# An encoder trunk on one core: the norms at the four stage borders done by halves of the tokens

## The chip and the metric

The kernel runs on one core of a Trainium2 chip. The metric is the device time of one execution in microseconds; the number to be predicted is the median over several executions.

## What is computed

Two layers over 1024 tokens of width 1024 in float32. Each layer is a token mixer and a gated MLP, both added to the residual stream x, with an RMS norm ahead of each; one last norm ends the trunk. Layer 0 mixes with multi-head latent attention, layer 1 with differential attention.

```python
def rmsnorm(x, g=None):
    x32 = x.astype(jnp.float32)
    y = x32 * lax.rsqrt(jnp.mean(x32 * x32, axis=-1, keepdims=True) + NORM_EPS)
    ...

def conv_ffn(h, w_up, conv_w, conv_b, w_down):
    u = h @ w_up                              # 1024 -> 2 x 2816
    ...                                       # depthwise convolution, width 3
    g, val = jnp.split(u, 2, axis=-1)
    return (jax.nn.silu(g) * val) @ w_down

def reference(...):
    for i in range(DEPTH):                    # DEPTH = 2
        h = rmsnorm(x, attn_norm_g[i])
        x = x + mixer(h)                      # mla_mixer, then diff_mixer
        x = x + conv_ffn(rmsnorm(x, ffn_norm_g[i]), ...)
    return rmsnorm(x, final_norm_g)
```

## The kernel before

The stream x lies in SBUF as eight tiles k of 128 features by 1024 tokens; a half is 512 tokens (left, right). Each engine has its own instruction order, written out by hand, with semaphores between; there is no scheduler. A product in float32 takes three matmuls (`passes`, `three_passes`): each operand is split into a high part, rounded by ScalarE (ACT) (`split_high`, `norm_high`), and a low part, the difference, taken by GpSimd (POOL) or VectorE (DVE) (`split_low`, `norm_low`; of the norm's tiles POOL has the even ones and DVE the odd ones).

The stages are: latent attention; the projection of its output (`project_phase`, tiles named `mo_`); the MLP (`ffn_phase`, `ffn_ps` is its PSUM); differential attention; its projection (`do_`); the second MLP; the final norm (`fin_`). Between two stages stands a barrier of all engines. The stage borders that the change touches are numbered 1 (projection `mo_` to MLP 0), 2 (MLP 0 to differential attention), 3 (projection `do_` to MLP 1) and 4 (MLP 1 to the final norm). At each the same chain runs: last product; last residual add (DVE); its square (ACT); square sums over the 128 partitions by matmuls with ones (L272, `norm_sum_halves`); mean (L212), root (ACT L177), reciprocal (L218), both on columns of 128 tokens; the change of stage; a spread of these values over the partitions by matmuls with the identity (L285, `norm_spread`); and then, tile by tile, scale (DVE L231), high part (ACT L183), low part (L196), each half of a tile for itself, left halves first. The first product waits for tile 0.

The projection makes eight output tiles m; `unit(m)` does the left half's 24 matmuls, then the right half's. During its last tiles ACT and POOL also prepare the next stage's up weights (`UpAhead`: the value's tile, the gate's tile, and the sums S1, S2, S4 of weight blocks, added by POOL at L704, L707 and L710). x is written to DRAM as it is finished (`spill`).

The MLP goes through 22 pairs of output tiles. The first pair is an ordinary product over eight k (`first_pair`, left halves of both tiles first). From the second on, blocks are combined by a scheme with seven products in place of eight: it needs sums and differences T1 to T4 of blocks of normed x (DVE L1143, high parts on ACT L957, low parts on DVE L1133 and POOL L1070) and of weight blocks (`block_high` L715 on ACT, `block_low` L720 on POOL). These start when the whole norm is done. The down projection runs in 11 steps g (`groups`); a step has 16 units of six matmuls, one for each output tile and half, each added to x by DVE (L1200). Behind the last step ACT squares, POOL adds the squares and splits the next stage's first weights.

The stage calls end at the barriers that the trace shows as L2738 (into MLP 0), L2743, L2750 and L2754.

## Time and profile before

| | |
|---|---|
| median of three runs | 2862.83 us |
| the runs | 2861.6, 2862.83, 2864.22 us |
| the profiled execution, its span | 2863.4 us |
| TensorE (PE) busy | 2741.2 us, 96% |
| VectorE (DVE), ScalarE (ACT), GpSimd (POOL) busy | 1779.9, 1355.9, 1455.6 us |
| DMA | 195.37 MB, 68 GB/s |

The profile is one execution. Its page gives busy times by engine; the trace behind it gives every instruction with its start, its duration, and what ended the idle time before it. Every time in this text that starts with "at" is a moment of this execution, in us from its start.

### The profile page before, as it was taken

The page shows a single profiled execution, that of the slowest core. Times are in us where ns is not written, and L with a number is a line of the kernel's source. Part 1 is how long each engine was busy: PE and PEld are TensorE (multiplying, and loading weights), DVE is VectorE, ACT ScalarE, POOL GpSimd, SP SyncE. Part 2 cuts the span into 40 slices and gives each one's busy share as a digit, 9 for nine tenths or more (in the row PEclk, how much of TensorE's full clock was granted, in tenths as well). Part 3 has the DMA queues.
Part 4 walks back from the last instruction along what each step waited for, and adds up shares of the span by engine and source line. Part 5 has one row for each costly group of instructions (what it writes and reads, how often), then busy time and mean ns, then how long its engine had stood idle before and what let it go on. Part 6 is the DMA issues. An engine that isn't in the chain of part 4 may idle for free. (4 is left out here: it accounts for less than half of the span.)

```text
span 2863.4 us, 40261 instructions
## 1 busy us (share of the span) xinstructions
PE 2741.2 (96%) x13708; PEld 2306.7 (81%) x13708; DVE 1779.9 (62%) x2481; ACT 1355.9 (47%) x2102; POOL 1455.6 (51%) x1119
## 2 busy tenths in 40 slices
PE   8999999999989999999989999999898999999998
PEld 6788888877878888788868888887787788887886
DVE  6577777773654554555478888888527545545555
ACT  5477777773444444311246665665414444443112
POOL 2355555552587777643543333332226877774443
PEclk9999999999999999999999999999899999999998
DMA  3000000003122222523020000000321212225221
GB/s 137 23 9 11 9 7 7 17 1 135 72 89 72 82 88 88 198 89 117 15 113 23 30 30 31 30 23 24 153 96 35 105 68 86 88 79 215 88 88 59
DMA packets 54395, 195.37 MB, mean 68 GB/s; under 512 B 6544, under 2 KB 9872, under 8 KB 53776
## 3 DMA queue, kind: packets, MB, share of 16 engines
q1 hardware_dynamic: 54288, 193.95, 18.6%
q8 instruction: 66, 1.08, 0.1%
q14 instruction: 41, 0.34, 0.0%
HBM read 148.84 MB, written 45.09 MB: 68 GB/s over the span
## 5 line engine op out<-in xcount | busy, mean ns | idle before, releaser
L1209 PE MATMUL ffn_ps<-ffn_b_hi,weights_hi 128*128 128x512 f32 x704 | 277.5, 394 | 20.1 <-POOL weights_lo L720 11.7
L1210 PE MATMUL ffn_ps<-ffn_b_lo,weights_hi 128*128 128x512 f32 x704 | 276.1, 392 | 0.0
L1211 PE MATMUL ffn_ps<-ffn_b_hi,weights_lo 128*128 128x512 f32 x704 | 275.8, 392 | 0.0
L360 POOL TENSOR_TENSOR weights_lo<-weights_raw,weights_hi 128x1024 fp32r<-128x1024 f32 (+2 forms) x65 | 127.5, 1967 | 216.3 <-ACT weights_hi L355 216.2
L1100 POOL TENSOR_TENSOR ffn_y_lo<-ffn_y_raw,ffn_y_hi 128x1024 fp32r<-128x1024 f32 x44 | 109.1, 2498 | 229.4 <-ACT ffn_y_hi L1030 229.4
L720 POOL TENSOR_TENSOR up_local_lo<-up_sums,up_local_hi 128x512 fp32r<-128x512 f32 x126 | 171.2, 1362 | 96.9 <-ACT up_local_hi L715 96.9
L2301 ACT ACTIVATE dif_p<-dif_s,dif_neg_max 128x1024 f32<-128x1024 f32 x128 | 142.1, 1113 | 124.9 <-DVE dif_neg_max L2487 114.5
L1209 PE MATMUL ffn_ps<-ffn_b_hi,up_local_hi 128*128 128x512 f32 x504 | 196.1, 389 | 0.0
L1210 PE MATMUL ffn_ps<-ffn_b_lo,up_local_hi 128*128 128x512 f32 x504 | 196.1, 389 | 0.0
L1211 PE MATMUL ffn_ps<-ffn_b_hi,up_local_lo 128*128 128x512 f32 x504 | 196.1, 389 | 0.0
L1030 ACT ACTIVATE ffn_y_hi<-ffn_y_raw 128x1024 fp32r<-128x1024 f32 x44 | 44.2, 1052 | 315.0 <-PE ffn_ps L1211 315.0
L1200 DVE TENSOR_TENSOR x_first<-x_first,ffn_ps 128x512 f32<-128x512 f32 x176 | 120.4, 687 | 111.9 <-PE ffn_ps L1211 111.9
L1200 DVE TENSOR_TENSOR x_second<-x_second,ffn_ps 128x512 f32<-128x512 f32 x176 | 120.4, 687 | 111.9 <-PE ffn_ps L1211 111.9
L715 ACT ACTIVATE up_local_hi<-up_sums 128x512 fp32r<-128x512 f32 x126 | 79.0, 632 | 230.2 <-PE ffn_ps L1211 150.4
L1853 DVE TENSOR_REDUCE mat_row_max<-lat_s 128x1 f32<-128x1024 f32 x128 | 156.2, 1220 | 39.4 <-PE lat_s L371 38.3
L1706 ACT ACTIVATE mat_pt_hi<-mat_turn 128x512 fp32r<-128x512 f32 x256 | 138.8, 594 | 85.6 <-PE mat_turn L1979 85.4
L2390 POOL TENSOR_TENSOR dif_q_lo<-dif_rotated,dif_q_hi 64x512 fp32r<-64x512 f32 x64 | 85.0, 1329 | 177.0 <-ACT dif_q_hi L2283 173.2
L1209 PEld LDWEIGHTS ffn_ps<-ffn_b_hi,weights_hi 128*128 128x128 f32 x704 | 133.3, 189 | 51.6 <-issue 16.6
L1868 DVE TENSOR_TENSOR mat_pt_lo<-mat_turn,mat_pt_hi 128x512 fp32r<-128x512 f32 x256 | 162.7, 678 | 4.8 <-ACT mat_pt_hi L1706 4.8
L1148 DVE SCALAR_TENSOR_TENSOR ffn_conv<-ffn_ps,vecs,ffn_conv 128x1023 f32<-128x1023 f32 x88 | 112.6, 1280 | 83.9 <-ACT ffn_conv L961 83.9
L2487 DVE TENSOR_REDUCE dif_neg_max<-dif_s 128x1 f32<-128x1024 f32 x128 | 150.4, 1215 | 22.4 <-PE dif_s L2603 22.4
L1798 POOL TENSOR_TENSOR mat_passed<-mat_inv_sum 128x1 f32<-128x1 f32 x128 | 24.9, 195 | 263.7 <-DVE mat_inv_sum L1861 263.7
(353 smaller groups left out, 8528.8 us busy)
## 6 DMA issues: line engine op xcount, KB each, us to landing
weights_raw<-in_up SPq DMA_DIRECT2D x44, 512.0 KB, 3.5
up_raw<-in_up SPq DMA_DIRECT2D x44, 512.0 KB, 4.1
ffn_products<-ffn_conv SPq DMA_DIRECT2D x44, 512.0 KB, 2.7
ffn_y_raw<-ffn_products SPq DMA_DIRECT2D x44, 512.0 KB, 4.1
ffn_down_raw<-in_down SPq DMA_DIRECT2D x24, 512.0 KB, 6.5
weights_raw<-in_diff_qkv SPq DMA_DIRECT2D x23, 512.0 KB, 3.5
weights_raw<-in_down SPq DMA_DIRECT2D x20, 512.0 KB, 6.0
x_spill<-x_in SPq DMA_DIRECT2D x16, 512.0 KB, 4.1
```

Source lines behind the costliest of these rows:

```text
L360: pool.tensor_tensor(w.lo[:], w.raw[:], w.hi[:].bitcast(F32), ALU.subtract).then_inc(w.lo_done, 1)
L720: pool.tensor_tensor(w.lo[name], w.block_raw(par, name), w.hi[name].bitcast(F32), ALU.subtract).then_inc(w.lo_done, 1)
L1148: dve.scalar_tensor_tensor(cv[:, 1:SEQ], pr[:, 0:SEQ - 1], vec(V_CONV_W + 2 * FT * 3 * layer, s, q), cv[:, 1:SEQ], ALU.mult, ALU.add).then ...
L1200: dve.tensor_tensor(xm, xm, bank(DOWN_BANKS[n % NACC]), ALU.add).then_inc(acc_added, 1)
L1209: pe.matmul(out, hi, x_hi, start=start, stop=False, skip_group_check=True)
L1210: pe.matmul(out, hi, x_lo, start=False, stop=False, skip_group_check=True)
L1211: return pe.matmul(out, lo, x_hi, start=False, stop=stop, skip_group_check=True)
L1706: act.activation(pt[:, 4 * half:4 * half + 4, (t % 2) * P:(t % 2 + 1) * P], turn_ps[half][:].rearrange("p (k m) -> p k m", m=P), ACT.Copy) ...
L1853: dve.tensor_reduce(row_max[:, col:col + 1], s_ps[t % 2][:], AX_X, ALU.max, negate=True).then_inc(max_ready, 1)
L1868: dve.tensor_tensor(pt_lo[b][part], turn_ps[half][:].rearrange("p (k m) -> p k m", m=P), pt_hi[b][part].bitcast(F32), ALU.subtract).then_i ...
L2301: act.activation((p0, p1)[m][t % 2][:], s_ps[m][:], ACT.Exp, bias=neg_max[:, col:col + 1], accum_out=total).then_inc(exp_done, 1)
L2487: dve.tensor_reduce(neg_max[:, col:col + 1], s_ps[m][:], AX_X, ALU.max, negate=True).then_inc(max_ready, 1)
```

## The change

1. Projection: tiles 5, 6 and 7 are done left halves first, then right halves (`TAIL`, `half_unit`). The left halves' square sum is taken in the middle of (5, right), the spread after it (`half_sum`, `half_spread`), and scale, high and low parts of all eight left tiles are done within the projection. ACT's and POOL's preparation of the up weights is cut into parts between them (`split_value`, `split_sums`, `split_gate`; `split_low_early`, `split_low_gate`). The first left scale waits until the left half of x has been written to DRAM, since the scale goes into the same place.
2. MLP: its first pair starts at once on left halves. The last right tile's add, square and square add stand at the start of the MLP; the right half's sum stands behind k=2 and its spread behind k=4 of the first pair.
3. Down projection: steps 9 and 10 are done by quarters (9 left, 10 left, 9 right, 10 right; 32 units j). The left sum stands behind unit 17, its spread behind unit 19, and all left scales and high and low parts among the right units. DVE, not POOL, adds the squares. The next stage's two weight splits are moved in ACT and POOL between the norm's parts (`split_high(..., only)`), and the first waits for the end of quarter 3. The last adds and the right norm stand in the next stage: in attention, sum in the middle of the first product K0, spread behind it, and then Q0.
4. Final norm: the left half is scaled and stored during quarters 3 and 4; the last stage has the right half alone.
5. Places: the normed x, in one buffer of 14 parts (`x_parts`), lies where `hh` and `hl` are; these are now kept half by half. The load of y for step 1 waits for product P5 and not P6.

The core of the diff:

```diff
+def half_sum(pe, nm, total, added, ones, out):
+    pe.wait_ge(nm.sq_added, added)
+    for t in range(4):
+        mm = pe.matmul(out[:, t:t + 1], total[:, t * P:(t + 1) * P], ones[:, 0:1],
+                       start=(t == 0), stop=(t == 3), skip_group_check=True)
+    mm.then_inc(nm.sq_summed, 1)
...
+def half_spread(pe, nm, ident, half, out):
+    pe.wait_ge(nm.rstd_ready, half + 1)
+    for t in range(4):
+        mm = pe.matmul(out[:, t * P:(t + 1) * P], half_cols(nm, half)[:, t:t + 1].to_broadcast([P, P]),
+                       ident, start=(t == 0), stop=(t == 3), skip_group_check=True)
+    mm.then_inc(nm.spread, 1)
...
@@ project_phase, ACT
-            for m in range(KT - 4, KT - 1):
-                square(m)
-            ahead.split_high(act, slots)
...
-            norm_root(act, out_norm)
+            square(WHOLE - 1)
+            square_half(WHOLE, 0)
+            ahead.split_value(act)
+            square_half(WHOLE + 1, 0)
+            ahead.split_sums(act)
+            square_half(WHOLE + 2, 0)
+            half_root(act, out_norm, 0)
+            square_half(WHOLE, 1)
+            for k in range(6):
+                norm_high(act, out_norm, k, 0)
+            square_half(WHOLE + 1, 1)
+            ahead.split_gate(act, slots)
+            for k in range(6, KT):
+                norm_high(act, out_norm, k, 0)
...
@@ project_phase, POOL
-            ahead.split_low(pool)
+            ahead.split_low_early(pool)
+            for k in (0, 2, 4):
+                norm_low(pool, out_norm, k, 0, out_norm.lo_even)
+            ahead.split_low_gate(pool)
+            norm_low(pool, out_norm, 6, 0, out_norm.lo_even)
...
@@ project_phase, PE
             first_units()
-            for m in range(2, KT):
+            for m in range(2, WHOLE):
                 unit(m)
-            norm_sum_halves(pe, out_norm, ones, KT, KT + 1)
+            for m in range(WHOLE, KT):
+                half_unit(m, 0)
+            half_unit(WHOLE, 1, lambda: half_sum(pe, out_norm, sq_acc[:, 0:HALF], tail_no(KT - 1, 0) + 2, ones, left_sums))
+            half_spread(pe, out_norm, ident, 0, left_rstd)
+            for m in range(WHOLE + 1, KT):
+                half_unit(m, 1)
...
@@ ffn_phase, DVE
-            norm_dve(dve, nm)
+            dve.tensor_tensor(last_tile, last_tile, last_product, ALU.add).then_inc(last_added, 1)
+            dve.wait_ge(nm.sq_ready, KT + 3)
+            dve.tensor_tensor(right_total, right_total, last_square, ALU.add).then_inc(nm.sq_added, 1)
+            half_mean(dve, nm, 1, right_sums)
+            half_rstd(dve, nm, 1)
+            for k in range(KT):
...
+                norm_scale(dve, nm, k, 1)
...
@@ ffn_phase, DVE, down projection
+            steps_before_tail(dve, lambda g, s, m: add_down(g))
+            for j in range(KT):
+                add_tail(j)
+            for m in range(KT):
+                add_tail(KT + m)
+                if m >= 2:
+                    half_add(dve, out_norm, squares, m - 1)
...
+            for k in range(1, KT):
+                norm_scale(dve, out_norm, k, 0)
+                if k > 1:
+                    add_tail(2 * KT + 2 + k)
+                if k % 2 == 0:
+                    left_low(k - 1)
...
@@ ffn_phase, PE
-            norm_spread(pe, nm, cst[:, C_IDENT:C_IDENT + P])
...
                     mm = first_pair(s, k, 0, (BANK_A[0], BANK_D)[s])
+                if k == 2:
+                    half_sum(pe, nm, right_total, KT + 4, ones, right_sums)
+                if k == 4:
+                    half_spread(pe, nm, cst[:, C_IDENT:C_IDENT + P], 1, right_rstd)
...
-            groups(pe, project_down)
-            norm_sum_halves(pe, out_norm, ones, 2 * KT - 2, 2 * KT - 1)
+            steps_before_tail(pe, project_down)
+            for j in range(4 * KT):
+                project_tail(j)
+                if j == 2 * KT + 1:
+                    half_sum(pe, out_norm, squares.total(0), KT - 1, ones, bank(LEFT_SUMS))
+                if j == 2 * KT + 3:
+                    half_spread(pe, out_norm, cst[:, C_IDENT:C_IDENT + P], 0, bank(LEFT_RSTD))
...
@@ diff_attention_phase, PE
-            norm_spread(pe, nm, cst[:, C_IDENT:C_IDENT + P])
-            project(0, K0, wkv, 0)
+            project(0, K0, wkv, 0, lambda: half_sum(pe, nm, squares.total(1), 2 * KT - 2, ones, right_sums))
+            half_spread(pe, nm, cst[:, C_IDENT:C_IDENT + P], 1, s_ps[1][:, HALF:SEQ])
```

Three places show the order. The first is DVE's at border 1, from the last tiles of the projection `mo_` into the MLP. Before the change (L571 adds squares, L566 adds the last tile's product to x, L231 scales, L196 takes a low part):

```order
L557 TENSOR_TENSOR x_in_4689<-x_in_4689,mo_acc 128x1024
L571 TENSOR_TENSOR mo_sq_acc<-mo_sq_acc,mo_sq 128x1024 x2
L566 TENSOR_TENSOR x_in_4689<-x_in_4689,mo_acc 128x512
L571 TENSOR_TENSOR mo_sq_acc<-mo_sq_acc,mo_sq 128x512
L566 TENSOR_TENSOR x_in_4689<-x_in_4689,mo_acc 128x512
L212 TENSOR_SCALAR ffn_norm_stat<-mo_total 128x8
L218 RECIPROCAL ffn_norm_stat<-ffn_norm_stat 128x8
L444 UNCONDITIONAL_BRANCH
L1122 UNCONDITIONAL_BRANCH
L231 SCALAR_TENSOR_TENSOR x_in_4689<-x_in_4689,vecs,ffn_ps 128x512 x3
```

With the change (L704 adds squares, L693 adds a product to x, L348 and L358 are mean and reciprocal, L235 scales, L200 takes a low part), all before the change of stage:

```order
L704 TENSOR_TENSOR mo_sq_acc<-mo_sq_acc,mo_sq 128x512 x2
L348 TENSOR_SCALAR ffn_norm_stat<-mo_total 128x4
L358 RECIPROCAL ffn_norm_stat<-ffn_norm_stat 128x4
L693 TENSOR_TENSOR x_in_4691<-x_in_4691,mo_acc 128x512
L235 SCALAR_TENSOR_TENSOR x_in_4691<-x_in_4691,vecs,mo_total 128x512 x2
L704 TENSOR_TENSOR mo_sq_acc<-mo_sq_acc,mo_sq 128x512
L235 SCALAR_TENSOR_TENSOR x_in_4691<-x_in_4691,vecs,mo_total 128x512
L200 TENSOR_TENSOR up_x_parts<-x_in_4691,up_x_parts 128x512
L235 SCALAR_TENSOR_TENSOR x_in_4691<-x_in_4691,vecs,mo_total 128x512 x2
L200 TENSOR_TENSOR up_x_parts<-x_in_4691,up_x_parts 128x512
L235 SCALAR_TENSOR_TENSOR x_in_4691<-x_in_4691,vecs,mo_total 128x512
L693 TENSOR_TENSOR x_in_4691<-x_in_4691,mo_acc 128x512
```

The left norm's scales and low parts have moved ahead of the branch into the next stage, between the adds of the right tiles.

The second is TensorE's, the last product of the projection and the start of the MLP. Before (L371 is the third pass of a product, L272 the square sums, L285 the spread, L1209 the first pass of the first pair):

```order
L371 MATMUL mo_acc<-hh,weights_lo 128x512
L272 MATMUL mo_total<-ones,mo_sq_acc 128x1 x8
L272 MATMUL mo_total<-ones,mo_sq 128x1 x4
L444 UNCONDITIONAL_BRANCH
L1206 UNCONDITIONAL_BRANCH
L285 MATMUL ffn_ps<-cst,ffn_norm_stat 128x128 x8
L1209 MATMUL ffn_ps<-ffn_b_hi,weights_hi 128x512
L1210 MATMUL ffn_ps<-ffn_b_lo,weights_hi 128x512
```

With the change (L450 and L1470 to L1472 are passes, L337 is a half's sum, L365 its spread; two stretches of passes are left out):

```order
L450 MATMUL mo_acc<-hh,weights_lo 128x512
L539 UNCONDITIONAL_BRANCH
L1467 UNCONDITIONAL_BRANCH
L1470 MATMUL ffn_ps<-up_x_parts,weights_hi 128x512
...
L1472 MATMUL ffn_ps<-up_x_parts,up_value_lo 128x512
L337 MATMUL ffn_ps<-ones,mo_sq_acc 128x1 x4
L1470 MATMUL ffn_ps<-up_x_parts,weights_hi 128x512
...
L1472 MATMUL ffn_ps<-up_x_parts,up_value_lo 128x512
L365 MATMUL ffn_ps<-cst,ffn_norm_stat 128x128 x4
L1470 MATMUL ffn_ps<-up_x_parts,weights_hi 128x512
```

The products start without a sum or spread ahead of them; those of the right half stand behind 18 and 30 passes.

The third is ACT's in the end of the first down projection, border 2. Before (L1035 splits the last down weights, L355 the next stage's, L1062 squares, L177 is the root):

```order
L1035 ACTIVATE ffn_down_hi<-ffn_down_raw 128x1024 x2
L355 ACTIVATE weights_hi<-weights_raw 128x1024 x2
L1057 ACT_TABLE_LOAD
L1057 ACTIVATE ffn_warm<-ones 128x1
L1062 ACTIVATE ffn_sq<-x_first 128x512 x16
L177 ACTIVATE diff_norm_stat<-diff_norm_stat 128x8
```

With the change (L318 squares, L353 is the root, L187 takes high parts of the norm, L434 splits the next stage's weights):

```order
L1257 ACT_TABLE_LOAD
L1257 ACTIVATE ffn_warm<-ones 128x1
L318 ACTIVATE ffn_sq<-x_first 128x512 x8
L353 ACTIVATE diff_norm_stat<-diff_norm_stat 128x4
L187 ACTIVATE hh<-ffn_left_scaled 128x512 x4
L434 ACTIVATE weights_hi<-weights_raw 128x1024
L187 ACTIVATE hh<-ffn_left_scaled 128x512
L434 ACTIVATE weights_hi<-weights_raw 128x1024
L318 ACTIVATE ffn_sq<-x_first 128x512
L187 ACTIVATE hh<-ffn_left_scaled 128x512
L318 ACTIVATE ffn_sq<-x_first 128x512
L187 ACTIVATE hh<-ffn_left_scaled 128x512
```

The two weight splits have moved from ahead of the squares to behind four high parts, and squares of the right half alternate with high parts of the left.

## Rows read from the trace of the kernel before

**Rows 1.** The page: span, busy time by engine

```profile
span 2863.4 us, 40261 instructions
...
PE 2741.2 (96%) x13708; PEld 2306.7 (81%) x13708; DVE 1779.9 (62%) x2481; ACT 1355.9 (47%) x2102; POOL 1455.6 (51%) x1119
```

**Rows 2.** Busy by stretch, borders 1 to 4 (x instructions, then clock)

```profile
741.87:751.27 9.40, 6.49 (x42) 6.17 (x40) 3.93 (x7) 2.73 (x5) 3.17 (x3) 0.68 0.47 167
1428.72:1440.00 11.28, 7.59 (x42) 7.13 (x41) 3.93 (x7) 2.92 (x6) 3.08 (x4) 0.70 0.37 122
2156.20:2164.71 8.51, 5.50 (x41) 5.18 (x40) 3.92 (x7) 2.73 (x5) 3.15 (x3) 0.82 0.49 179
2842.09:2863.40 21.31, 7.58 (x41) 7.10 (x40) 11.68 (x19) 1.02 (x3) 1.47 (x2) 0.63 0.51 197
```

**Rows 3.** Timeline, border 1: start, us, engine, line, tiles [idle before <-releaser]

```profile
741.87 1.84 PE L272 MATMUL mo_total<-ones,mo_sq_acc 128*128 128x1 f32 x16
...
742.79 0.63 ACT L530 ACTIVATE mo_sq<-x_in 128x512 f32<-128x512 f32 x1 [4.80 <-DVE x_in L566]
...
743.57 1.03 PE L272 MATMUL mo_total<-ones,mo_sq 128*128 128x1 f32 x8
...
746.27 3.76 PE L285 MATMUL ffn_ps<-cst,ffn_norm_stat 128*128 128x128 f32 x16 [1.67 <-PEq L2738]
...
751.27 0.76 PE L1209 MATMUL ffn_ps<-ffn_b_hi,weights_hi 128*128 128x512 f32 x1 [1.24 <-POOL ffn_b_lo L196]
```

**Rows 4.** Timeline, PE: a product in the projection, and a spread amid products

```profile
725.55 0.39 PE L369 MATMUL mo_acc<-hh,weights_hi 128*128 128x512 f32 x1
...
95.69 1.95 PE L285 MATMUL lat_s<-cst,lat_stat 128*128 128x128 f32 x16
```

**Rows 5.** Timeline, POOL, in the end of the projection

```profile
725.26 1.29 POOL L710 TENSOR_TENSOR up_sums<-up_raw,up_sums 128x512 f32<-128x512 f32 x1
...
741.28 2.36 POOL L360 TENSOR_TENSOR weights_lo<-weights_raw,weights_hi 128x1024 fp32r<-128x1024 f32 x1
```

**Rows 6.** Timeline, POOL and DVE where they meet, or DVE reads PSUM

```profile
710.62 3.41 POOL L360 TENSOR_TENSOR weights_lo<-weights_raw,weights_hi 128x1024 fp32r<-128x1024 f32 x1 [7.47 <-ACT weights_hi L355]
...
750.46 1.21 DVE L196 TENSOR_TENSOR ffn_b_lo<-x_in,ffn_b_hi 128x512 fp32r<-128x512 f32 x1
...
1197.30 3.06 DVE L1200 TENSOR_TENSOR x_first<-x_first,ffn_ps 128x512 f32<-128x512 f32 x5
```

**Rows 7.** Timeline, MLP 0 after its first pair, and (last row) MLP 1

```profile
765.33 0.69 DVE L196 TENSOR_TENSOR ffn_b_lo<-x_in,ffn_b_hi 128x512 fp32r<-128x512 f32 x1 [0.70 <-ACT ffn_b_hi L183]
766.24 4.63 DVE L1143 TENSOR_TENSOR x_in<-x_in 128x1024 f32<-128x1024 f32 x4 [0.21 <-DVE ffn_b_lo L196]
...
770.60 2.68 POOL L720 TENSOR_TENSOR weights_lo<-up_raw,weights_hi 128x512 fp32r<-128x512 f32 x2 [5.32 <-ACT weights_hi L715]
...
773.92 6.16 DVE L1133 TENSOR_TENSOR ffn_b_lo<-x_in,ffn_b_hi 128x1024 fp32r<-128x1024 f32 x2 [3.05 <-ACT ffn_b_hi L957]
...
794.01 0.47 PE L1209 MATMUL ffn_ps<-ffn_b_hi,weights_hi 128*128 128x512 f32 x1 [2.41 <-POOL weights_lo L720]
...
803.13 0.70 PE L1209 MATMUL ffn_ps<-ffn_b_hi,weights_hi 128*128 128x512 f32 x1 [3.42 <-POOL weights_lo L720]
...
2207.43 0.47 PE L1209 MATMUL ffn_ps<-ffn_b_hi,weights_hi 128*128 128x512 f32 x1 [2.48 <-POOL weights_lo L720]
```

**Rows 8.** Timeline, border 2

```profile
1408.30 4.77 POOL L360 TENSOR_TENSOR weights_lo<-weights_raw,weights_hi 128x1024 fp32r<-128x1024 f32 x2 [12.25 <-ACT weights_hi L355]
...
1440.00 0.47 PE L369 MATMUL dif_proj<-hh,weights_hi 128*128 128x512 f32 x1 [1.50 <-POOL hl L196]
...
1476.07 0.50 PE L2601 MATMUL dif_s<-dif_key,dif_q_hi 128*128 128x512 f32 x1 [0.62 <-DVE dif_key L2457]
```

**Rows 9.** Timeline and the page's DMA issues, border 4

```profile
2850.36 10.62 DVE L231 SCALAR_TENSOR_TENSOR fin_staging<-x_second,vecs,fin_rstd 128x512 f32<-128x512 f32 x16 [3.05 <-PE fin_rstd L285]
...
out<-fin_staging SPq DMA_DIRECT2D x16, 256.0 KB, 2.0
```

444 lines of the change are left out of this document (319 added, 125 removed).

## The prediction

> **What bounds the kernel now.** I read the page first: TensorE is busy 2741.2 of 2863.4 us, 96% [rows 1]. So nothing can be won but what TensorE idles or spends at the lower clock, and I looked for where that lies. The busy table by stretches answers it for the four borders that the change touches [rows 2]: 9.40, 11.28, 8.51 and 21.31 us pass between the last product of one stage and the first of the next (at the last border, the end), together 50.5 us with TensorE "busy" for 27.2 of them, most of that with tiny sums and spreads at a low clock. The timeline of border 1 shows the chain [rows 3]: square sums at 741.87, the last tile's at 743.57, its end at 744.60, then mean, root and reciprocal, the change of phase, the spread at 746.27, and the first product at 751.27, 9.40 after the last one. TensorE idles 1.24 us just before it and goes on at the granted clock .68 of the stretch, the mean of its two levels. That is the size of the prize. The question is what the same work costs where it goes.
>
> **Unit sizes.** I call T the start of the third half tile from a projection's end (one tile, one half of the tokens): 725.55 [rows 4]. In the kernel before that is (6, right), in the changed one (5, right). From there to 741.87 are 72 matmuls, 16.3 us, so 0.227 each, 5.44 a half tile; a down step's unit of six takes 1.36. A spread of 16 records takes 1.95 us amid products at full clock [rows 4]; half of one is 0.9 with its start, and a half sum I set at the same 0.9. DVE: a scale 0.66 (10.62 by 16) [rows 9], an add with a PSUM input 0.60 [rows 6], a subtraction of two SBUF tiles 0.69 alone, 0.61 in a row. ACT 0.63 for 512 columns [rows 3]. POOL 1.29 and 2.36 [rows 5].
>
> **What it costs in locks.** The second question was whether POOL's work, which grows in these tails, leaves DVE alone. The trace says no [rows 6]: DVE's subtraction of 512 columns begun in POOL's takes 1.21 instead of 0.69, and a POOL split of 1024 columns that meets DVE takes 3.41 instead of 2.36. Adds that read PSUM are untouched: five in 3.06 us. So each DVE operation on two SBUF tiles (square adds, low parts) waits for the POOL operation that runs, up to 1.29 or 2.36 us, and the reverse. Against a change that puts more of both kinds beside each other this speaks; by the rows a meeting costs 0.52 or 1.05 us (1.21 less 0.69, 3.41 less 2.36).
>
> The Trainium skill (page "SBUF — State Buffer", section "SBUF: two separate sides") has the pair of ports as an exclusive lock between GpSimd and such DVE operations, and the one that comes second blocks wholly. By it a meeting could cost a whole operation of the other, up to 2.36, and border 2 would end near the later of its two bounds below; by the two rows' extras, near the earlier. Which of these holds is for the trace after to show.
>
> **Borders 1 and 3, the projection's end.** Tiles 5, 6, 7 go left first. The left sum stands in (5, right) at k=4, at T+2.7 by products alone. It needs three left squares and three square adds on DVE. The squares stand in ACT's queue around the up weights' splits; the split of the sums waits for POOL's last add of the sums, which ended at 726.55, T+1.0, in [rows 5] and comes at T+0.5 or so; after it POOL's low splits (2.4 and three of 1.3) alternate with the square adds. I get the sum at T+5.4: a stall of 2.7. (5, right) ends at T+9.1, the spread at T+10.0, the last product at T+16.4+0.9+0.9+2.7 = T+20.9. Meanwhile DVE scales from T+10.2; its queue (8 scales, 4 lows, two adds, two square adds, about 10 us with two locks) and POOL's (gate split, 2.36, behind ACT's square of (6, right) at T+18.0, then low 6) end near T+23.9. With a change of phase, 1.67 less the 0.7 of mean to reciprocal, thus 1.0, the first product comes at T+24.8, where it was T+25.7 (751.27) at border 1 and T+24.8 at border 3. So the left norm, done early, brings 0.9 and nothing: the phase now waits for DVE and POOL, not for the norm.
> Inside the first pair of the MLP, TensorE now has the right sum and the right spread (1.8 us), but is not slowed from 751 to 755 as before (some 2 us, of which I keep 1.4, since there is still a stall). The right norm: 30 matmuls 6.8, sum 0.9, spread after k=4 to 8.7, perhaps 0.6 of low clock; scales from 9.5, eight at 0.66 with four lows between, and ACT and POOL behind them as in the old pace of about 1.03 per tile: the end 18.9 behind the first product, T+43.7. Before it was 766.02, T+40.5 [rows 7].
> This matters because of what comes next. [Rows 7] give the chain: four differences on DVE from 766.24 (1.16 each), a wait of 3.05 for ACT, low parts from 773.92, convolutions, and at the end TensorE waiting 2.41 us at 794.01 for a low weight part. Being 3.2 late uses up the 3.05; POOL's two low splits, at 770.60 just after DVE's differences, now fall beside them and each costs DVE 1.3, 2.6 together. Sum: 3.2+2.6-3.05 = 2.8, with the later pairings 3.1. So the product at 794.01 (T+68.5) comes at T+71.6: **loss 3.1**. At border 3 the same wait stands at 2207.43 (2.48 us); there nothing is won at the start, **loss 4.0**. Ends: if the locks fall well, 0.7 and 1.5; if, besides, the stall of 5 to 6 us before that product brings the low clock, 4.8 and 5.7. Waits of 2.41 and 2.48 kept the clock (next matmul 0.47 long), that of 3.42 lost it (0.70) [rows 7]; the loss then partly hides in the next wait, so I don't add it to the likeliest.
> Edits that cost nothing: the spills by halves (SP has only them there, and the left ones are on their way when the first scale comes), the other places of the parts of x (same sizes), and the earlier wait before the load of y for step 1.
>
> **Border 2, down projection to attention.** T2 = 1428.72 - 16 x 1.36 = 1406.96 is the start of the right halves. Left sum two units later, spread after two more: scales from T2+7.4. From there DVE has 8 scales, 11 adds, 4 lows, 3 square adds, 16.1 us; last unit of TensorE at 21.8+1.8 = 23.6, so without any lock DVE would end at 24.9 and K0's first product come at T2+26.9. But the next weights' splits (4.77 us on POOL for two) [rows 8], which used to lie in the open at 1408.30, now stand behind the end of quarter 3 in ACT and between the low parts in POOL, and the squares 8 to 10 ahead of high parts 5 to 7. Op by op I get DVE's end at T2+29.3 and K0 at T2+31.0 (29.0 if DVE gets in ahead of the second split), against 1440.00, T2+33.0 [rows 8]. The right norm then stands inside K0 and Q0: its end K0+19.6 = T2+50.6, before 50.4; what TensorE waits for next, at 1476.07, is the key's rotation on DVE 0.62 [rows 8]. So of 2.0 won at K0 little is left unless the norm's end comes too; the product of lambdas, 1.4 us on DVE ahead of the rotation, no longer waits, 1.1. **Gain 1.5**, from -1 to +4; 6 without locks.
>
> **Border 4, the end.** T4 = 2842.09 - 21.76 = 2820.33. TensorE's end 21.8+1.8 = T4+23.6; change of phase 1.0; last add, square and four square adds 3.1; sum 1.0; mean to reciprocal 0.7; half a spread at the lower clock 2.0; eight scales 5.3 of the 10.62 [rows 9]; last store, from the end of the scales 2860.98 to the end of the span, 2.4; latencies between these, 0.9. Sum 40.0, 2860.3 against 2863.4: **gain 3.0** (2 to 3.5). Half of the scales went under the products, and the norm's chain with its adds stays. The 16 stores of 256 KB take 2.0 each [rows 9]; only the last counts.
>
> **Sum.** -3.1 -4.0 +1.5 +3.0 = -2.6: 2.6 us slower than the profiled 2863.4. That execution is 0.6 above the median of 2862.83, so 2865.4; I say 2865. That is within 0.2% (5.7 us), about what a measurement can tell from no change.
>
> **Rivals.** *The cover works (faster).* The squares and low parts find gaps between POOL's operations, DVE gets in first, and the chain after the right norm has more slack than I take. Then the four borders give what their stalls held: 3.2 at border 1 (5 us of idle and low clock less 1.8 for sum and spread), 1.8 at border 3, 6 at border 2, 3 at the end: 14 us, 2849. For it: ACT is half idle, the lock costs one operation at a time, and the idle was real. Against: [rows 6], and that TensorE waited at 794.01 for a chain that begins with the norm's end. It decides if the norm ends before T+40.5: chance 0.24.
> *Locks and clock (slower).* The left sum's stall and the longer wait before 794.01 go beyond what kept the clock: 4.8 and 5.7 lost, border 2 gives -1, the end +2: 9.5 slower, 2872. It begins where a wait passes about 3 us, between 2.48 and 3.42 of [rows 7]. Chance 0.30.
> *Little moves* (the forecast): chance 0.46.
>
> **Range.** From 2853, which leaves out the best part of the first rival, to 2873, which takes in the second. Faster by over 0.2% 0.24, within 0.46, slower 0.30.
>
> **What would show it.** Right: in the projection's end a TensorE wait of 2 to 3 us for the left square sum; first MLP product at T+24.8; right norm's end at T+43 to 44; a wait of 5 to 6 us at the product that was at 794.01; K0 some 2 us earlier; the end of the run about 3 us shorter after the last product. Wrong: low parts and square adds on DVE at 0.69 beside POOL; a wait at that product of 2.4 or less; or a new wait elsewhere, for a buffer or a spill, that I set at nothing.

## The result

Six runs of the changed kernel have a median of 2874.27 us (2867.74 to 2875.32), six of the kernel before 2863.19 (2859.53 to 2864.89). The ratio is 1.0033 with a 95% interval of 1.0023 to 1.0042: 0.33%, or 9.4 us, slower. (The two medians lie 11.1 us apart: four of the changed kernel's six runs are at 2874 to 2875 us, two at 2868.) The likeliest value of the prediction was 2.6 us slower; what came is close to its second rival, 9.5 us, at the upper end of the range, 2873: the ratio gives 2872.6, just inside, and the median of 2874.27 lies just outside.

The profiled execution of the changed kernel, page and busy table by stretches (last product of a stage to first of the next; after the change there is no sum or spread in between, except at border 4):

```profile
span 2873.5 us, 40106 instructions
...
PE 2745.3 (96%) x13676; PEld 2305.9 (80%) x13676; DVE 1806.9 (63%) x2527; ACT 1357.9 (47%) x2110; POOL 1422.9 (50%) x1089
```

```profile
748.48:752.30 3.82, 0.16 (x1) 0.03 (x1) 3.03 (x3) 0.00 (x0) 2.11 (x2) 1.00 0.00 0
1438.25:1443.44 5.19, 0.16 (x2) 0.03 (x1) 3.57 (x7) 2.48 (x4) 0.00 (x0) 0.95 0.00 0
2165.35:2169.26 3.91, 0.16 (x2) 0.03 (x1) 3.06 (x3) 0.00 (x0) 2.13 (x2) 1.00 0.00 0
2856.21:2873.50 17.29, 4.11 (x17) 3.56 (x16) 9.06 (x15) 1.03 (x3) 0.00 (x0) 0.59 0.31 121
```

The stretches of [rows 2] have shrunk from 9.40, 11.28, 8.51 and 21.31 us to 3.82, 5.19, 3.91 and 17.29. In sum that is 20.3 us less at the borders. Seven pairs of half sum and half spread now stand in the stages, some 1.85 us each, 13 us; that would leave a gain of 7, and yet the run is 10 us longer. So some 17 us more went into the stages. Matching the products one for one (start of a product now, less its start before) shows where:

| stretch, us | before, three profiles | changed, two profiles | difference of the means |
|---|---|---|---|
| border 1: last matmul ahead of T to the 901st product matmul of MLP 0 | 243.49, 243.45, 243.42 | 248.40, 248.56 | +5.0 |
| border 2: first down product to first score product | 289.53, 289.31, 289.81 | 290.04, 290.60 | +0.8 |
| border 3: as border 1, MLP 1 | 242.51, 243.39, 243.51 | 248.29, 250.07 | +6.0 |
| border 4: first down product to the end | 263.52, 264.28, 264.19 | 262.98, 261.58 | -1.7 |
| the rest of the attentions (before T of border 1; first scores to T of border 3) | 1388.9, 1385.6, 1381.5 | 1388.4, 1381.1 | -0.6 |

The borders give +10.1; the two stretches left out, the rest of the up projections, take 217.7 us each in every profile. The last row is work that the change doesn't touch; it differs by 7 us between executions of one kernel, so the borders' stretches are a better measure than single totals.

Two things fill border 1's stretch, in the first profile of each kernel: TensorE idles 15.2 us where it idled 11.6, and its products lose 7.3 us at the lower clock where they lost 4.0 (by their pitch, the time from one start to the next, above 0.227). Sums and spreads take 3.3 instead of 6.5.

The timeline of the changed kernel at border 1:

```profile
726.53 0.39 PE L448 MATMUL mo_acc<-hh,mo_third_hi 128*128 128x512 f32 x1
...
731.31 1.05 PE L337 MATMUL mo_total<-ones,mo_sq_acc 128*128 128x1 f32 x8 [1.90 <-DVE mo_sq_acc L704]
...
736.66 1.05 PE L365 MATMUL mo_total<-cst,ffn_norm_stat 128*128 128x128 f32 x8
...
746.53 2.39 POOL L439 TENSOR_TENSOR weights_lo<-weights_raw,weights_hi 128x1024 fp32r<-128x1024 f32 x1 [1.64 <-ACT weights_hi L434]
...
747.53 1.94 DVE L200 TENSOR_TENSOR up_x_parts<-x_in,up_x_parts 128x512 fp32r<-128x512 f32 x1 [0.77 <-ACT up_x_parts L187]
...
748.88 1.71 POOL L200 TENSOR_TENSOR up_x_parts<-x_in,up_x_parts 128x512 fp32r<-128x512 f32 x1
749.39 1.74 DVE L704 TENSOR_TENSOR mo_sq_acc<-mo_sq_acc,mo_sq 128x512 f32<-128x512 f32 x1
...
752.30 0.47 PE L1470 MATMUL ffn_ps<-up_x_parts,weights_hi 128*128 128x512 f32 x1 [3.66 <-PEq L3054]
...
754.91 0.63 PE L1472 MATMUL ffn_ps<-up_x_parts,weights_lo 128*128 128x512 f32 x1
...
758.10 0.95 PE L337 MATMUL ffn_ps<-ones,mo_sq_acc 128*128 128x1 f32 x8
...
761.76 1.05 PE L365 MATMUL ffn_ps<-cst,ffn_norm_stat 128*128 128x128 f32 x8
...
771.64 0.69 DVE L200 TENSOR_TENSOR up_x_parts<-x_in,up_x_parts 128x512 fp32r<-128x512 f32 x1 [0.70 <-ACT up_x_parts L187]
772.54 6.84 DVE L1370 TENSOR_TENSOR x_in<-x_in 128x1024 f32<-128x1024 f32 x4 [0.21 <-DVE up_x_parts L200]
779.30 6.77 DVE L1360 TENSOR_TENSOR up_x_parts<-x_in,up_x_parts 128x1024 fp32r<-128x1024 f32 x2
...
774.22 4.07 POOL L888 TENSOR_TENSOR weights_lo<-up_raw,weights_hi 128x512 fp32r<-128x512 f32 x2 [2.64 <-ACT weights_hi L883]
...
794.53 0.47 PE L1470 MATMUL ffn_ps<-up_x_parts,weights_hi 128*128 128x512 f32 x1 [2.09 <-DVE ffn_conv L1378]
...
799.92 0.47 PE L1470 MATMUL ffn_ps<-up_x_parts,weights_hi 128*128 128x512 f32 x1 [2.38 <-POOL weights_lo L888]
```

(5, right) starts at T = 726.53. The left sum waits 1.90 us and stands at T+4.8; after it the pitch of matmuls goes from 0.23 to 0.43 and each is 0.63 long, the lower of the clock's two levels, and (5, right) takes until 736.66, the spread. Behind the last product (748.48) DVE's last low part and square add lie in POOL's gate split and low part: 1.94 and 1.74 us for what takes 0.6 to 0.7. They end at 751.13 and TensorE has waited 3.66. The clock falls once more, at about 753.5 (a matmul of 754.91 is 0.63 long), so that sum and spread of the right half come at 758.10 and 761.76, and the norm ends at 772.33, 5.3 us later after T than before ([rows 7] has 766.02). Then the four differences, beside POOL, take 6.84 instead of 4.63, and the wait of 794.01 in [rows 7] stands at 799.92, with a new one of 2.09 us ahead of it.

Borders 2 and 4 in the same execution:

```profile
1192.41 0.47 PE L1470 MATMUL ffn_ps<-ffn_y_hi,ffn_down_hi 128*128 128x512 f32 x1 [2.66 <-POOL ffn_down_lo L1325]
...
1194.43 0.63 PE L1471 MATMUL ffn_ps<-up_x_parts,weights_hi 128*128 128x512 f32 x1
...
1443.44 0.76 PE L448 MATMUL dif_proj<-hh,weights_hi 128*128 128x512 f32 x1 [5.03 <-PEq L3059]
...
1460.60 0.58 ACT L2551 ACTIVATE dif_plain<-dif_proj 128x512 f32<-128x512 f32 x1
...
1461.38 0.76 PE L448 MATMUL dif_proj<-hh,weights_hi 128*128 128x512 f32 x1 [3.47 <-issue]
...
1482.45 0.39 PE L2901 MATMUL dif_s<-dif_key,dif_q_hi 128*128 128x512 f32 x1
...
2855.77 0.63 ACT L318 ACTIVATE ffn_sq<-x_second 128x512 f32<-128x512 f32 x1 [0.73 <-DVE x_second L1433]
...
2857.97 3.07 DVE L329 TENSOR_TENSOR ffn_sq<-ffn_sq 128x512 f32<-128x512 f32 x4
...
2861.09 1.86 PE L337 MATMUL fin_ps<-ones,ffn_sq 128*128 128x1 f32 x8 [4.72 <-DVE ffn_sq L329]
...
2865.78 5.36 DVE L235 SCALAR_TENSOR_TENSOR fin_staging<-x_second,vecs,fin_ps 128x512 f32<-128x512 f32 x8 [2.17 <-PE fin_ps L365]
```

At border 2 K0 starts 5.03 us after TensorE's last product, and TensorE waits 3.47 at 1461.38, ahead of its third product, for ACT to take the second one out of PSUM (1460.60), which stands behind seven high parts of the right norm; the first scores come at 1482.45. The clock is at its lower level from 1459.96 to 1466.78. At border 4 the last square (2855.77) holds back the change of stage, and four square adds in a row, 3.07 us, the right sum. At 1192.41, the start of the down projection, stands the wait of 2.66 us that the kernel before has too at 1186.54; here the clock falls after it.

### The profile page after: what moved, and what is told of

Read it like the earlier page. It is cut to its first block and busy times, and to the rows that moved or that the text cites. A ratio compares the mean times of both kernels' runs of the same rounds, so it can differ in the third digit from the quotient of the medians.

```text
span 2873.5 us, 40106 instructions
## 1 busy us (share of the span) xinstructions
PE 2745.3 (96%) x13676; PEld 2305.9 (80%) x13676; DVE 1806.9 (63%) x2527; ACT 1357.9 (47%) x2110; POOL 1422.9 (50%) x1089
## 5 line engine op out<-in xcount | busy, mean ns | idle before, releaser
L1470 PE MATMUL ffn_ps<-up_x_parts,weights_hi 128*128 128x512 f32 x704 | 280.2, 398 | 26.9 <-POOL weights_lo L888 8.3
L1472 PE MATMUL ffn_ps<-up_x_parts,weights_lo 128*128 128x512 f32 x704 | 277.7, 395 | 0.0
L1471 PE MATMUL ffn_ps<-up_x_parts,weights_hi 128*128 128x512 f32 x704 | 277.7, 394 | 0.0
L1470 PE MATMUL ffn_ps<-up_x_parts,up_local_hi 128*128 128x512 f32 x504 | 196.6, 390 | 0.0
L1471 PE MATMUL ffn_ps<-up_x_parts,up_local_hi 128*128 128x512 f32 x504 | 196.3, 390 | 0.0
L1472 PE MATMUL ffn_ps<-up_x_parts,up_local_lo 128*128 128x512 f32 x504 | 196.1, 389 | 0.0
L1470 PEld LDWEIGHTS ffn_ps<-up_x_parts,weights_hi 128*128 128x128 f32 x704 | 134.5, 191 | 61.1 <-issue 23.6
L448 PE MATMUL dif_proj<-hh,weights_hi 128*128 128x512 f32 x368 | 150.3, 408 | 8.6 <-PEq L3059 5.0
L1472 PEld LDWEIGHTS ffn_ps<-up_x_parts,weights_lo 128*128 128x128 f32 x704 | 134.4, 191 | 28.6
L1471 PEld LDWEIGHTS ffn_ps<-up_x_parts,weights_hi 128*128 128x128 f32 x704 | 134.8, 192 | 27.5
```

The costliest lines, as they stand in the source:

```text
L448: pe.matmul(out, w_hi, x_hi, start=start, stop=False)
L1470: pe.matmul(out, hi, x_hi, start=start, stop=False, skip_group_check=True)
L1471: pe.matmul(out, hi, x_lo, start=False, stop=False, skip_group_check=True)
L1472: return pe.matmul(out, lo, x_hi, start=False, stop=stop, skip_group_check=True)
```

## Experiments

Each number of a stretch below is a border's, as in the table, from one profile of the kernel named: +1.0 means 1.0 longer than the mean of the three profiles of before (243.45, 289.55, 243.14 and 264.00).

**One half of the change at a time.** The first kernel takes back the projections' ends and the starts of both MLPs:

```diff
-            for m in range(WHOLE, KT):
-                half_unit(m, 0)
...
+            norm_sum_halves(pe, out_norm, ones, KT, KT + 1)
... in the MLP
-                if k == 2:
-                    half_sum(pe, nm, right_total, KT + 4, ones, right_sums)
...
+            norm_spread(pe, nm, cst[:, C_IDENT:C_IDENT + P])
```

> The changed kernel with the projections' ends and the start of both MLPs as before the change; the down projections' quarters, the norms after them and the new places of buffers stay. If the loss was made at borders 1 and 3 (read off the trace after: +4.9 and +5.8 us) and the down projections' borders gave back 1.1 and 0.6, this kernel takes 1 to 2 us less than the kernel before, 2861 to 2862. Rival: the new places of the buffers or the quarters cost the time; then it stays near 2870.

Measured: 2860.05 us, ratio 0.9982 (0.9972 to 0.9993). Borders +0.1, +1.9, -0.6, -2.4. The rival, that the places of the buffers or the quarters cost the time, falls. The borders give 1.0 less in sum, as expected; the ratio gives 5 less (2 to 8), and the rest of that is in no border. Border 2's +1.9 holds 2.9 us of low clock at the start of the down projection.

The second takes back the down projections' quarters and the norms behind them, by putting `groups(...)`, `norm_sum_halves` and `norm_spread` back there.

> The other half: only the projections' ends and the starts of the MLPs changed; the down projections and the norms after them as before. If borders 1 and 3 make the loss, 10 to 11 us over the kernel before, about 2874. Rival, the loss is elsewhere: under 2867.

Measured: 2876.94 us, ratio 1.0048 (1.0032 to 1.0064). Borders +5.2, +3.6, +5.2, -0.1. So the loss is made at borders 1 and 3; the rival falls. Border 2 has its old order here and still +3.6: 1.6 of it is the low clock at the start of the down projection, and the rest stands between K0 and the first scores, 38.5 us instead of 36.1, where the clock falls at a wait of 2.84 us (1468.38) and stays low for 6.8; in the profile of before it held there after 2.48 (1463.26).

**The right norm earlier.**

```diff
-                if k == 2:
+                if k == 1:
                     half_sum(pe, nm, right_total, KT + 4, ones, right_sums)
-                if k == 4:
+                if k == 2:
                     half_spread(pe, nm, cst[:, C_IDENT:C_IDENT + P], 1, right_rstd)
```

> The changed kernel, but in each MLP's first pair the right half's sum stands behind k=1 and its spread behind k=2 (before: 2 and 4), 6 and 12 matmuls earlier. If the late end of the right norm makes the waits in the first pairings (it ended 6.3 us later than before the change), the norm ends 2.7 us earlier in each MLP at full clock and each MLP gains 2 to 3: 4 to 6 us less than the changed kernel, 2867 to 2870. Rival: those waits hang on the low clock and on the first pairs' products, not on the norm; then no change beyond 1 us.

Measured: 2865.14 us, ratio 1.0005 (0.9995 to 1.0015), 8 us less than the changed kernel by the two ratios. Borders 1 and 3: +1.0 and +1.3. Its timeline:

```profile
726.60 1.05 PE L337 MATMUL mo_total<-ones,mo_sq_acc 128*128 128x1 f32 x8 [2.21 <-DVE mo_sq_acc L704]
...
727.83 0.40 PE L449 MATMUL mo_acc<-hl,mo_third_hi 128*128 128x512 f32 x1
...
745.99 0.47 PE L1470 MATMUL ffn_ps<-up_x_parts,weights_hi 128*128 128x512 f32 x1 [3.68 <-PEq L3054]
...
762.58 0.69 DVE L200 TENSOR_TENSOR up_x_parts<-x_in,up_x_parts 128x512 fp32r<-128x512 f32 x1 [0.70 <-ACT up_x_parts L187]
...
763.48 5.74 DVE L1370 TENSOR_TENSOR x_in<-x_in 128x1024 f32<-128x1024 f32 x4 [0.21 <-DVE up_x_parts L200]
```

The norm ends 17.3 us after the first product (763.27 less 745.99), where it was 20.0 in the changed kernel: 2.7 earlier, as expected. Less of POOL's work now falls on the four differences (5.74). The gain, 4.0 and 4.7, is larger than the 2 to 3 expected: at border 1 the left sum's wait (2.21) was followed by full clock in this execution (0.40 long at 727.83), about 1.3 us of it. At border 3 the left sum kept the clock in the changed kernel's first profile too, and against that one the gain is 3.8: 2.7 for the norm, and a stretch of low clock later in the pairings is half as long. That a norm's end moves the MLP this much shows the chain of the prediction.

**The left sum later.**

```diff
-            half_unit(WHOLE, 1, lambda: half_sum(pe, out_norm, sq_acc[:, 0:HALF], tail_no(KT - 1, 0) + 2, ones, left_sums))
-            half_spread(pe, out_norm, ident, 0, left_rstd)
-            for m in range(WHOLE + 1, KT):
-                half_unit(m, 1)
+            half_unit(WHOLE, 1)
+            half_sum(pe, out_norm, sq_acc[:, 0:HALF], tail_no(KT - 1, 0) + 2, ones, left_sums)
+            half_unit(WHOLE + 1, 1, lambda: half_spread(pe, out_norm, ident, 0, left_rstd))
+            half_unit(WHOLE + 2, 1)
```

> The changed kernel, but the left half's sum stands behind the whole of (5, right) and its spread in the middle of (6, right). If the stall of 1.9 us at the sum and the low clock after it (3.9 us of it, about 1.8 lost) hold the projection up, TensorE ends about 3.5 us earlier and, the spread coming at T+10 and not at T+11.6, the first product of the MLP 1.5 us earlier at each border: 3 less than the changed kernel, 2871. Rival: DVE and POOL end the phase whatever TensorE does; then no gain, or up to 1 us of loss.

Measured: 2869.15 us, ratio 1.0022 (1.0012 to 1.0033). That is 3 us less than the changed kernel by the ratios, the size that was expected, but the two intervals overlap. Borders 1 and 3: +5.1 and +4.4; for the changed kernel +5.0 and +6.0. At border 1:

```profile
741.72 1.90 DVE L200 TENSOR_TENSOR up_x_parts<-x_in,up_x_parts 128x512 fp32r<-128x512 f32 x1 [0.76 <-ACT up_x_parts L187]
743.54 1.75 DVE L704 TENSOR_TENSOR mo_sq_acc<-mo_sq_acc,mo_sq 128x512 f32<-128x512 f32 x1
...
746.45 0.76 PE L1470 MATMUL ffn_ps<-up_x_parts,weights_hi 128*128 128x512 f32 x1 [6.34 <-PEq L3054]
```

The stall is gone and the products end 3.7 us earlier after T (2.4 at border 3). But DVE's last operations, again in POOL's (1.90, 1.75), end only 1.1 earlier: the wait ahead of the first product grows to 6.34 us, and its first matmul is slow at once (0.76). At border 3 the first product comes 0.3 us later after T than in the changed kernel's first profile. By the borders this is mostly the rival: DVE and POOL end the phase, and the time that TensorE no longer waits in (5, right) it waits there, with a longer stretch of low clock behind.

**Both.** The two edits together.

> Both moves together: the right half's sum and spread behind k=1 and k=2 of the MLP's first pair, the left half's sum behind the whole of (5, right). The first alone brought borders 1 and 3 from +4.9 and +5.8 to +1.0 and +1.9 us against the kernel before; the second alone made the MLP's first product 1 us earlier but brought nothing behind the first pairings. If it is the end of the right norm that counts, and the first product moves it one for one, the two add up: borders 1 and 3 at 0 and +1, the whole 1 to 2 us under the first move alone. Rival: once the norm ends about when it did before the change, the chain hangs on the first pair's products and on ACT, as before; then borders stay at +1 and +2.

Measured: 2863.19 us, ratio 1.0006 (0.9997 to 1.0015). Borders 1 and 3: +3.2 and +1.8, worse than the first edit alone at border 1. They don't add up, and at border 1 the rival (+1) isn't met either.

```profile
751.60 0.77 PE L1470 MATMUL ffn_ps<-up_x_parts,weights_hi 128*128 128x512 f32 x1 [6.38 <-PEq L3054]
...
756.43 0.63 PE L1472 MATMUL ffn_ps<-up_x_parts,up_value_lo 128*128 128x512 f32 x1
756.86 1.12 PE L337 MATMUL ffn_ps<-ones,mo_sq_acc 128*128 128x1 f32 x8
...
769.19 0.69 DVE L200 TENSOR_TENSOR up_x_parts<-x_in,up_x_parts 128x512 fp32r<-128x512 f32 x1 [0.70 <-ACT up_x_parts L187]
```

After 6.38 us of waiting the clock is still low at 756.43, and the right sum comes 5.3 us after the first product; with the first edit alone, after a wait of 3.68, it came after 4.4. The norm ends 18.3 after the first product and not 17.3. So the earlier products turned into a longer wait and that into low clock.

**And DVE's square add ahead of its wait**, on top of both:

```diff
                 if k == 5:
                     add_half(WHOLE + 1, 1)
+                if k == 6:
+                    add_square_half(WHOLE + 1, 1)
             left_low(KT - 1)
-            add_square_half(WHOLE + 1, 1)
```

> As e5, and DVE adds the square of (6, right) between the seventh scale and the eighth, ahead of the wait for the last high part, and not as its last operation. In the changed kernel the last low part took 1.94 us and that square add 1.74, both beside POOL. If DVE's lock with POOL sets the end of the projection, the phase ends about 1 us earlier, and the MLP's first product too. Rival: POOL's own chain (gate split, then low part 6) ends last; then 0.5 or nothing.

Measured: 2867.41 us, ratio 1.0010 (1.0001 to 1.0019). The first product comes 0.5 us earlier after T at both borders, borders +3.1 and +1.4; POOL's low part 6 ends last now. The rival, and by time nothing.

**Most of POOL's two operations taken away.**

```diff
             for name in ("A11", "A12"):
-                block_low(pool, blocks, 1, 1, name)
+                pool.wait_ge(hi_done, block_no(1, name))
+                pool.tensor_tensor(w_lo[name][:, 0, 0:32], block_raw(1, name)[:, 0, 0:32], ...).then_inc(lo_done, 1)
```

> The changed kernel, but POOL takes the low parts of the weight blocks A11 and A12 of pairing 1 for 32 columns of one of four tiles alone, in both MLPs; the rest of these parts is left out. It measures the lock: the four differences on DVE took 6.84 us beside these two operations and 4.63 before the change without them. If the lock costs what the rows say, they take 4.6 to 4.9 and, with the low parts behind them earlier, each MLP gains about 2: 4 us less than the changed kernel. Rival: the chain waits for something else behind them (ACT's high parts, products); then the four take 4.6 and the MLP gains less than 0.5.

Measured: 2867.59 us, ratio 1.0008 (0.9999 to 1.0017). Borders 1 and 3: +3.0 and +1.6.

```profile
772.07 4.75 DVE L1372 TENSOR_TENSOR x_in<-x_in 128x1024 f32<-128x1024 f32 x4 [0.21 <-DVE up_x_parts L200]
777.08 6.44 DVE L1362 TENSOR_TENSOR up_x_parts<-x_in,up_x_parts 128x1024 fp32r<-128x1024 f32 x2 [0.25 <-ACT up_x_parts L1155]
```

4.75 us for the four differences instead of 6.84: the two POOL operations cost DVE 2.1. At border 1 the stretch is 2.0 shorter than in the changed kernel, as expected, but this isn't shown to be the lock's alone: POOL has less to do itself and begins its next low parts 3.8 us after the norm's end, where it was 5.9. At border 3 the stretch is 3.5 and 5.3 shorter than in the two profiles, more than the edit was to give, and the waits in the later pairings fell otherwise there. The rival, a gain under 0.5, falls.

**The changed kernel again**, with two versions of the down projections' half on the same chip.

> The changed kernel once more, on the same chip as the two below. Its runs fell in two groups, 2868 (two of six) and 2874 to 2875 (four). If the low clock after a wait of 2.7 us at the start of each down projection (7 slow matmuls in the profile, none before the change) comes and goes between executions, the runs spread over some 7 us again, and the profile may show it at one, both or neither; the median stays 8 to 11 us over the kernel before. Rival: the change causes it; then both are slow in every profile of kernels that have it.

Measured: 2872.28 us, ratio 1.0030 (1.0017 to 1.0043), runs from 2869.14 to 2874.91, not in two groups. Its profile has +5.1 and +6.9 at borders 1 and 3. At the second down projection's start the clock holds this time. So the expectation of a fall that comes and goes is met for the second start; at the first it fell again. And at border 3 the same wait as in the first profile ends the other way (row of the sum and one of a matmul behind it, first this execution, then the first one):

```profile
2143.10 1.87 PE L337 MATMUL do_total<-ones,do_sq_acc 128*128 128x1 f32 x8 [2.01 <-DVE do_sq_acc L704]
...
2145.41 0.63 PE L449 MATMUL do_acc<-hl,do_third_hi 128*128 128x512 f32 x1
```

```profile
2149.78 1.05 PE L337 MATMUL do_total<-ones,do_sq_acc 128*128 128x1 f32 x8 [2.13 <-DVE do_sq_acc L704]
...
2151.01 0.40 PE L449 MATMUL do_acc<-hl,do_third_hi 128*128 128x512 f32 x1
```

2.01 us of waiting and a fall to 0.63 long matmuls until 2149.67; 2.13 us and none (0.40). The first product of MLP 1 comes 3.0 us later after T for it.

> The kernel with the projections' ends as before and the down projections' quarters (as e1), again: 2 to 5 us under the kernel before, 2858 to 2861. Rival: the first measurement was chance, and it lies within 1 us of the kernel before.

Measured: 2861.55 us, ratio 0.9988 (0.9977 to 1.0000). Borders +0.1, +1.9, -0.6, -2.5, which is 1.1 less in sum; the ratio says 3.4 less, as expected, with an interval that ends at no change.

**One square add ahead of the change of stage**, on top of that kernel:

```diff
                 if m < 5:
                     half_add(dve, out_norm, squares, KT + m - 1)
+            half_add(dve, out_norm, squares, 2 * KT - 4)
... in attention and in the final norm
-            for n in range(2 * KT - 4, 2 * KT):
+            for n in range(2 * KT - 3, 2 * KT):
                 half_add(dve, nm, squares, n)
```

> As e9, and DVE adds the fifth-last square (number 12 of 0 to 15) behind the last add of the down projection, ahead of the change of stage, where it waited for ACT's square of unit 30 for 0.7 us anyway; three square adds, not four, then stand ahead of the right sum. At border 4 the chain after the change of stage was one last add and four square adds, 3.7 us, where the prediction took 3.1 from the last product on: the end comes 0.6 to 0.8 earlier after the last product, the total 0.6 to 1 less than e9. Rival: the change of stage comes later by as much as is won; no gain.

Measured: 2857.15 us, ratio 0.9981 (0.9969 to 0.9993), the lowest of all, though not told apart from the version without the edit.

```profile
2838.68 0.69 DVE L329 TENSOR_TENSOR ffn_sq<-ffn_sq 128x512 f32<-128x512 f32 x1
2840.37 0.69 DVE L2898 TENSOR_TENSOR x_second<-x_second,ffn_ps 128x512 f32<-128x512 f32 x1 [1.01 <-PEq L2991]
2840.97 2.28 DVE L329 TENSOR_TENSOR ffn_sq<-ffn_sq 128x512 f32<-128x512 f32 x3
...
2847.41 5.36 DVE L235 SCALAR_TENSOR_TENSOR fin_staging<-x_second,vecs,fin_ps 128x512 f32<-128x512 f32 x8 [2.17 <-PE fin_ps L365]
```

From the start of the last product to the end of the run 16.2 us are left, where e9 and the changed kernel have 17.6: 0.8 from the square add, 0.6 from a right sum at full clock for part of its time (1.29 us instead of 1.87). At the end the edit brings 1.4, more than the 0.6 to 0.8 expected; K0 doesn't move (5.38 after the start of the last product in both): ACT's last square ends the phase there in both, 1.2 us ahead of K0.

**The kernel before, two more profiles.** (The count in the first expectation is wrong: eleven profiles of kernels with the change or a part of it, the clock fell at the first start in all, at the second in eight.)

> The kernel before the change, for a second profile of it. At both starts of a down projection TensorE waits 2.7 us; in the profile of before the clock stayed full there, in nine profiles of kernels with the change or parts of it it fell at the first start every time and at the second six times of nine. If that fall is a matter of the single execution, this profile and the next show it at least once in four places; if the change brings it, never.

> As e11, a third profile of the kernel before: a fall at one of its two starts at the least if it is a matter of the single execution, none if the change brings it. Besides, the stretches that the change doesn't touch (latent attention ahead of border 1, differential attention) show how far executions of one kernel lie apart there; up to 5 us is what the profiles of the other kernels show.

Measured: 2863.70 and 2859.64 us. In both the clock holds at the first start and falls at the second, after the same 2.68 us:

```profile
1186.25 0.47 PE L1209 MATMUL ffn_ps<-ffn_y_hi,ffn_down_hi 128*128 128x512 f32 x1 [2.68 <-POOL ffn_down_lo L1106]
...
1187.02 0.39 PE L1209 MATMUL ffn_ps<-ffn_y_hi,ffn_down_hi 128*128 128x512 f32 x1
...
2597.23 0.47 PE L1209 MATMUL ffn_ps<-ffn_y_hi,ffn_down_hi 128*128 128x512 f32 x1 [2.68 <-POOL ffn_down_lo L1106]
...
2599.24 0.63 PE L1210 MATMUL ffn_ps<-ffn_b_lo,weights_hi 128*128 128x512 f32 x1
```

So the fall at the second start is a matter of the execution. At the first it fell in none of three profiles here and in eleven of eleven of the other kernels; the last section shows in what these differ. The stretch from the first scores to border 3's T is 663.6, 660.6 and 655.9 us in the three profiles of before.

## Why the prediction came out as it did

The likeliest value, 2.6 us slower and hardly to be told from no change, was wrong in size: it is 9.4 slower. The range held the measured ratio (2872.6) by its upper rival, and missed the median by 1.3 us.

**Borders 1 and 3.** The mechanism is the one described, step by step. The left sum came 0.6 us earlier than said, every later step 0.7 to 2.1 later. The left sum at T+4.8 (said 5.4), the spread's end at T+10.9 (10.0), the end of DVE's queue at T+24.6 (23.9), the first product at T+25.8 (24.8), the norm's end at T+45.8 (43.7), the product of 794.01 at T+73.4 (71.6). From the norm's end to that product it is 27.6 us, as in the sum (27.9). Two terms failed. The low clock was put at 0.6 us in the first pair; it is about 1.6 in (5, right), where it was not counted, and 1.6 behind the first product. And the phase's end lacks 0.7 us: DVE's last two operations, each beside one of POOL's, took 3.7. Losses 5.0 and 6.0 where 3.1 and 4.0 were said. That the long wait would stand at one product, 5 to 6 us, is wrong: it is spread over two, 2.09 and 2.38.

**The locks.** 2.6 us were said for two POOL operations on the four differences. 6.84 less 4.63 is 2.2, and taking most of POOL's work away gives 2.1. Of the two readings of the lock, border 2 ended near the earlier bound: K0 starts at T2+28.8 (T2 being 23.6 us ahead of 1438.25, the last product's end), where the rows' extras gave 29.0 and whole operations 31.0. But that is one place, and the prices of [rows 6] don't hold at border 1: the low part of 1.94 us cost 1.25 more than alone, not 0.52. It began inside POOL's split and ended at 749.47, 0.55 us after the split's end (748.92); the square add ended at 751.13, 0.54 us after POOL's low part (750.59). By the Trainium skill (page "SBUF — State Buffer", section "SBUF: two separate sides") the second one waits for the whole of the first, and at these two places the trace agrees. What a meeting costs is then what the other's operation still has to run, from nothing to all of it.

**Border 2.** The first scores come at T2+67.8, before at T2+69.1: 1.3 gained (said 1.5). That it is so close is luck. K0 came 4.2 us earlier and not 2.0, and 2.9 of it went again before the scores, in the wait of 3.47 us at 1461.38 and the low clock around it, which the prediction didn't have. And the stretch as a whole is 0.8 longer, since the clock falls at the first down product, 1.6 us (the 3.66 us that the down projection takes longer are 1.88 of sum and spread and, for the most part, this). That cost had no term.

**Border 4.** From T4 (23.6 us ahead of 2856.21) to the end 40.9, said 40.0, before 43.1: 2.2 gained of 3.0. The other two profiles of the kernel before have 42.2 and 42.1, and against them it is 1.2 to 1.3; the prediction's own profile had the longest end of the three. The missing 0.9 is the last square of ACT ahead of the change of stage and the five adds, 3.7 us and not 3.1 with the sum at the lower clock.

**The rivals.** "Locks and clock" came true in its size, 9.5, and in its mechanism as to the fall of the clock at the left sum. Beyond that the size is luck: its wait of 5 to 6 us never came, and what border 2 lost (0.8 in its stretch, where it said 1) came from the down projection's start and not from locks. Its threshold is refuted. It said that a wait decides between 2.48 and 3.42 us; at the left sums, in five profiles, the clock fell after 1.90, 2.00, 2.01, 2.02 and 2.12 us and held after 1.79, 1.92, 2.12, 2.13 and 2.21, so no length of wait divides them. "The cover works" fell: no border but the last gained in its stretch.

## What to carry to other kernels

A norm that is split in halves to shorten a border has two ends, and the next stage's first combined work waits for the second. Place its sum and spread as early in the first products as their inputs allow, and check what the later end pushes work into. A wait taken from TensorE in one place, while other engines end the phase, comes back at the barrier with more low clock behind it. And where VectorE and GpSimd both have SBUF operations in a tail, count the tail by the two queues together. Price a wait of about 2 us of TensorE as its length and, in part of the executions, a stretch of low clock behind it; no threshold can be read off one profile.

## What the runs showed of the hardware

A wait of TensorE of about 2 to 2.7 us is now followed by the lower clock and now not, in one kernel at one place: at the second down projection's start (2.68 us) it held in the first profile of the kernel before and fell in the two others; at border 3's left sum it held after 2.13 and fell after 2.01 us. Where it falls, some matmuls run at a pitch of 0.43 instead of 0.23, and 1.6 us are lost: from its first product to its last the second down projection of the kernel before takes 241.97 us where the clock held and 243.60 where it fell. (In the kernels with the down projections' half alone it is 14 matmuls and 2.9 us, at the first start.)

The length of such a wait doesn't tell which it will be, but its distance from the last rise of the granted clock, which the trace records, does in every case here. At the starts of the down projections (28 waits of 2.66 to 2.69 us in fourteen profiles) the clock held in seven, where the first product came 379.70 to 380.23 us (six) or 377.33 us (one) after the last rise. It fell in the other 21, at 372.29 to 374.42 and at 378.61 to 379.58 us. At the left sums (ten waits) it fell 73.49 to 73.69 and 88.74 us after the last rise and held at 75.49 and at 89.02 to 89.08. So a wait's place in the clock's own course decides, as far as these 38 waits show; the bands were read off afterwards, and no run was made to try them.

This covers the first start too. The kernel before comes to it 379.70 to 380.23 us after the last rise in all three profiles; the three profiles with the down projections' half alone come at 379.53 to 379.58, and the other eight at 372.29 to 374.42 or at 378.73 and 379.00. Its second start it reached at 380.15 (held), 374.15 and 374.07 us (fell). Why the half alone comes 0.1 to 0.7 us sooner is not shown.

The Trainium skill (page "TensorE: Matmul & The Clock Gate", section "Part 1: The HAM clock gate") says that what the chip looks at runs free of the program, so that one kernel differs between executions; that agrees with the second start.

The stretch from the first scores of differential attention to its projection, which no version changes, took 654.99 to 663.6 us in fourteen profiles, and this goes with the lower clock: 37.5, 30.7 and 20.5 us at the lower level in the three profiles of before (663.6, 660.6 and 655.9 us), 17.1 in the shortest.
